# Thirty seven-product units in five downs, their first weight sum made in HBM by GpSimd's DMAs

## The chip, the core and the metric

The program runs on one core of one Trainium2 chip. The metric is the device time of one execution in microseconds, the median of three runs. A profiled execution gives the trace: its span is the time from the first to the last instruction, and its own time is given beside it.

## The reference, cut to what matters

Two transformer blocks follow one another on 256 tokens of width 1024, in float32. The first has a mixer (an RWKV part and a differential attention part, joined by gates), a feed-forward part with a squared ReLU and a gated embedding. The second has two layers, each with a half-weighted SwiGLU, an attention and a second half-weighted SwiGLU:

```python
x = x + jnp.square(jax.nn.relu(h @ w_ff1[i])) @ w_ff2[i]          # first block: 4096 rows of w_ff2
...
x = x + FFN_RES_WEIGHT * swiglu(rms_norm(x, norm_ffn1[layer]), ...)   # swiglu: (silu(x@gate) * (x@up)) @ down
x = x + mixed @ w_out[layer]
x = x + FFN_RES_WEIGHT * swiglu(rms_norm(x, norm_ffn2[layer]), ...)   # down: 2816 rows
```

The five long downs of the title are `w_ff2` (32 contraction tiles of 128) and the four `w_down` (22 tiles each); their output is 256 tokens by 1024 columns and is added to X.

## The kernel before, in words

**Pieces.** All weights stream through SBUF in the order of `stream_plan`, as pieces of 128 x 2048 float32 (1 MB). Piece j is loaded into `raw[j % 3]` by SyncE (`next_raw`, L3681), rounded to float32r on ScalarE into `hi[j % 3]` (L2688, script entry "hi"), and VectorE subtracts to get `lo[j % 3]` (L3067, entry "lo"). A product of activations and weights is three matmuls, high by high, high by low and low by high (`mm3`, L2179 to L2181). The cast of piece j waits until piece j-3 has been used, and the load of piece j+3 is issued when the low part of piece j is done. Each engine executes its entries in the order of one script, which a planner writes out when the program is built; the mixers and attentions are woven by it from several tracks, the feed-forward parts and downs run straight.

**A down.** `rows_into_x` takes the pieces of a down two contraction tiles at a time (pairs 0, 1, 2, ...), then two tail pieces of four tiles by 512 columns each. A pair is 256 rows of weights by 1024 columns, and the tokens come in two halves of 128: eight products of 128 tokens by 128 rows by 512 columns, 24 matmuls of 512 columns.

**Units.** For the pairs in `SEVENS` (`seven_piece`) the same result is made as a two by two block product with seven products (a Strassen-Winograd scheme) in place of eight. It needs three sums of activation blocks and three of weight blocks, each with a high and a low part:
- the token sums are made in the up projection or first feed-forward matrix, right after VectorE has the activations: `mix` (L3046 to L3051), a cast on ScalarE (L2673), `mix_lo` (L3059);
- the weight sums are made from the raw piece. With the piece's four blocks w0 to w3 of 512 columns, entry "w_sums" (L3086 to L3091) makes w3-w1, overwrites w1 in the raw buffer by w1-w0 (the block of product 5), then w3-(w1-w0) and w2 minus that. The piece's own cast therefore waits for the second of these four. ScalarE rounds the three sums (L2692, "w_hi"), VectorE subtracts (L3095, "w_lo").

The order of the products of a unit is "3127645", in the last unit of a down "1267543"; 6, 7 and 4 use the weight sums. Products 1, 5, 6 and 7 are accumulated over all units of a down in four banks of their own, and after the last unit `sevens_out` adds them into X (a copy on ScalarE, L2695, and eight instructions on VectorE, L3106 to L3124). The sums of weights lie in sets of buffers, two for the `w_down` ("a") and one for `w_ff2` ("s"), taken in turn; `used` makes a sum wait for the last unit of its set, and `after` for the matmuls that read what lay there before. In "a", `sums_early` emits the sums of the next unit before the low part of the piece ahead of it.

**GpSimd** does little: after each norm's squares it makes the reciprocal roots (entry "n_root", L3654 to L3660), for which VectorE waits at L3163 before it makes the rows of token factors. The first norm's root is made at 17 to 21 us, the second one's near 252 us, after the first mixer.

Of the kernel before, what the change touches and what calls it, by code (L numbers as in the profile page):

```python
# [30 lines left out]
SEVENS = {"a": (1, 3, 4, 6, 7), "s": (3, 5, 7, 9, 11)}  # L31
# [191 lines left out]
def program(nc, ws, xin, xtin, pin, colsin, constin, smallin, rowin, out):  # L223
# [4 lines left out]
    with ExitStack() as ctx:  # L228
# [10 lines left out]
        x_in = [[sem(f"x_in{b}{h}") for h in range(2)] for b in range(2)]  # L239
        raw_in = [sem(f"raw_in{i}") for i in range(NRAW)]  # L240
# [254 lines left out]
        class Sevens:  # L495


            def __init__(self, n, acts, sums, mixed, parts):
                self.H, self.L = acts
                self.sums = [(ar_([128, 3, 512], R), ar_([128, 3, 512], R), ar_.again([128, 3, 512])) for ar_ in sums]  # L500
                self.ML = [mixed([128, 3, 128], R) for _ in range(n)]
                self.MS = [mixed.again([128, 3, 128], i) for i in range(n)]
                self.MH = [mixed([128, 3, 128], R) for _ in range(n)]
                self.parts = [t[:, :, :].rearrange("p a n -> p (a n)") for t in parts]

        by_src = {"a": Sevens(5, (aH, aL), [Arena(14 * 4096), Arena(h_at - arena0)], Arena(17 * 4096), (sgm[0], sgm[1], sgs[0])),
                  "s": Sevens(5, (sH, sL), [Arena(h_at - arena0)], late_ar, (rl[0], rl[1], h_rest))}
# [5 lines left out]

        sevens = {}
        for i, (name, _, n, *_) in enumerate(plan):
            src = "a" if "_w_down_" in name else "s" if name == "w_ff2" else None
            if src and n // 2 in SEVENS[src]:
                sevens[i] = (src, SEVENS[src].index(n // 2))

# [90 lines left out]
        def emit_lo(j):  # L610
            if not weaving[0] and j + 1 in sevens and sevens[j + 1][0] == "a" and sevens[j + 1][1]:
                sums_early(j + 1)
            wanted["lo"].add(j)
            emit_wanted()
# [4 lines left out]
        def sums_early(j):  # L619

            if j in sevens and j not in summed:
                src, unit = sevens[j]
                sets = len(by_src[src].sums)
                in_h = unit == sets - 1
                summed[j] = [wsum_v.add() for _ in range(3)]
                emit("w_sums", dve=2.6, j=j, own=summed[j], used=sum(n < j for n in sevens) - min(unit, sets - 1),
                     after=freed[j - SEVENS[src][unit] - 1] if in_h else None)

        def split_hi():
# [3 lines left out]
            emit("hi", act=1.9, j=j, after=freed.get(j - NSPL), sums=summed[j][0] if j in sevens else None)  # L633
# [2015 lines left out]
        def scalar_program(e):  # L2649
# [27 lines left out]
            for s in script:  # L2677
                kind = s["kind"]
                sl = s.get("slot")
                if kind == "hi":  # L2680
                    j = s["j"]
                    e.wait_ge(raw_in[j % NRAW], 16 * (j // NRAW + 1))
                    if s["after"]:
                        e.wait_ge(s["after"][0], s["after"][1])
                    if s["sums"]:
                        e.wait_ge(wsum_v.sem, s["sums"])
# [310 lines left out]
        def vector_program(e):  # L2997
# [41 lines left out]
            def mix(mix_, a, made):  # L3039

                if mix_:
# [5 lines left out]
                    e.tensor_tensor(a[:, 0, second], a[:, 0, second], a[:, 1, second], ALU.add).then_inc(mix_v.sem, 1)  # L3047
# [3 lines left out]
                    e.tensor_tensor(z[:, 2, :], a[:, 1, first], z[:, 0, :], ALU.subtract).then_inc(mix_v.sem, 1)  # L3051
# [21 lines left out]
            for s in script:  # L3073
# [4 lines left out]
                elif kind == "w_sums":  # L3078
                    w = raw[s["j"] % NRAW][:, :].rearrange("p (q n) -> p q n", q=4)
                    e.wait_ge(raw_in[s["j"] % NRAW], 16 * (s["j"] // NRAW + 1))  # L3080
# [5 lines left out]
                    e.tensor_tensor(WS[:, 1, :], w[:, 3, :], w[:, 1, :], ALU.subtract)  # L3086
                    e.tensor_tensor(w[:, 1, :], w[:, 1, :], w[:, 0, :], ALU.subtract).then_inc(wsum_v.sem, 1)
                    e.wait_ge(wsum_v.sem, s["own"][0])
                    e.tensor_tensor(WS[:, 0, :], w[:, 3, :], w[:, 1, :], ALU.subtract).then_inc(wsum_v.sem, 1)
                    e.wait_ge(wsum_v.sem, s["own"][1])  # L3090
                    e.tensor_tensor(WS[:, 2, :], w[:, 2, :], WS[:, 0, :], ALU.subtract).then_inc(wsum_v.sem, 1)  # L3091
# [4 lines left out]
                elif kind == "seven_add":  # L3096
# [13 lines left out]
                    t = e.scalar_tensor_tensor(to[0, 1], banks[five.b][:, :], f[0], to[0, 1], ALU.mult, ALU.add)  # L3110
                    t.then_inc(seven_v.sem, 1)
                    ready(seven)
                    e.wait_ge(seven_v.sem, v[0])
                    e.tensor_tensor(w, banks[seven.b][:, :], u, ALU.add).then_inc(seven_v.sem, 1)
                    t = e.scalar_tensor_tensor(to[1, 1], banks[five.b][:, :], f[1], to[1, 1], ALU.mult, ALU.add)
                    t.then_inc(seven_v.sem, 1)
                    e.wait_ge(seven_v.sem, v[1])
                    t = e.scalar_tensor_tensor(to[0, 1], u, f[0], to[0, 1], ALU.mult, ALU.add)
                    t.then_inc(seven_v.sem, 1)
                    e.wait_ge(seven_v.sem, v[2])  # L3120
                    t = e.scalar_tensor_tensor(to[1, 0], w, f[1], to[1, 0], ALU.mult, ALU.add)
                    t.then_inc(seven_v.sem, 1)
                    e.wait_ge(seven_v.sem, v[3])
                    t = e.scalar_tensor_tensor(to[1, 1], w, f[1], to[1, 1], ALU.mult, ALU.add)  # L3124
# [500 lines left out]
        def gpsimd_program(e):  # L3625
# [20 lines left out]

            after_own(e.memset(st[:, 16:18], -0.5))
            for s in script:
                kind = s["kind"]
                sl = s.get("slot")  # L3650
                if kind == "n_root":
# [8 lines left out]
                    e.tensor_tensor(st[:, 14:16], st[:, 4:6], st[:, 4:6], ALU.mult).then_inc(factors.sem, 1)  # L3660
                elif kind == "f_roots":
# [13 lines left out]
        def sync_program(e):  # L3675
            def next_raw(j):

                if j + NRAW < len(plan):
                    i = j % NRAW
                    e.wait_ge(lo_ready, j + 1)  # L3680
                    e.dma_start(raw[i][:, :], ws[j + NRAW]).then_inc(raw_in[i], 16)  # L3681
# [126 lines left out]
```

## Time and profile before

| | |
|---|---|
| median of three runs | 1413.95 us (1413.87 to 1414.29) |
| the profiled execution's own time | 1413.19 us |
| its span | 1411.4 us |
| TensorE busy | 1403.6 us, 99% |
| VectorE, ScalarE, GpSimd busy | 1149.3 (81%), 817.8 (58%), 28.1 us (2%) |
| HBM read | 247.64 MB, 176 GB/s over the span |

Busy time is the union of an engine's instructions. Matmuls overlap in the trace (each is drawn 0.39 us long while the next starts earlier), so the price of a matmul is the distance between two starts. "Idle before" is put down to the engine whose event came last.

### The profile page before, as it was taken

The numbers are of one execution on the slowest core, as the hardware profiler recorded it, in microseconds if no ns is written. First come the engines' busy times: TensorE is split into PE (matmuls) and PEld (weight loads), VectorE is DVE, ScalarE is ACT, GpSimd is POOL, SyncE is SP. The second block draws the span as 40 slices with busy tenths as digits, with TensorE's granted clock in tenths as the row PEclk, the third lists the DMA queues.
The fourth block names the chain that finished last, engine by engine and source line by source line (L and its number), as shares of the span: only waits on it lengthen the run. The fifth ranks groups of instructions, "written<-read, shape, count | busy, mean of one in ns | idle before, by whom it ended". The sixth has DMA issues, their size and how long they took to land.

```text
span 1411.4 us, 22781 instructions
## 1 busy us (share of the span) xinstructions
PE 1403.6 (99%) x9163; PEld 1194.6 (85%) x9163; DVE 1149.3 (81%) x1601; ACT 817.8 (58%) x1110; POOL 28.1 (2%) x93
## 2 busy tenths in 40 slices
PE   8999999999999999999999999999999999999999
PEld 8988778888888888889878888888888887888887
DVE  6866776898877887988868888987889798688797
ACT  7745474655447655555766565555555557665562
POOL 1000000000001100000000000000000000000000
PEclk9999999999999999999999999999999999999999
DMA  9441325455555545455334555555545454355543
GB/s 357 163 150 63 115 102 203 179 179 209 199 211 179 209 180 192 167 207 200 135 117 176 182 199 187 209 179 190 198 179 201 163 176 147 113 203 191 182 176 120
DMA packets 37544, 250.15 MB, mean 177 GB/s; under 512 B 4288, under 2 KB 4416, under 8 KB 8384
## 3 DMA queue, kind: packets, MB, share of 16 engines
q1 hardware_dynamic: 37152, 248.51, 49.2%
q8 instruction: 73, 1.20, 0.3%
q10 hardware_dynamic: 288, 0.19, 0.1%
q14 instruction: 31, 0.25, 0.1%
HBM read 247.64 MB, written 1.05 MB: 176 GB/s over the span
## 4 chain that ended last, share of the span: by engine, by line
PE 97%; DMA 1%; ACT 0%; DVE 0%; SPq 0%; issue 0%; DVEq 0%; ACTq 0%
PE ps L2260 24%; PE ps L2179 16%; PE ps L2181 16%; PE ps L2180 15%; PE ps L2267 13%; PE ps L2432 2%; PE ps L2244 1%; PE ps L2248 1%; PE ps L2250 1%; DMA raw<-ws 1%; PE ps L2344 1%; PE ps L2645 1%; PE ps L2625 1%; PE ps L2634 1%; PE ps L2417 0%; PE ps L2569 0%
## 5 line engine op out<-in xcount | busy, mean ns | idle before, releaser
L3067 DVE TENSOR_TENSOR lo<-raw,hi 128x2048 fp32r<-128x2048 f32 (+1 forms) x230 | 522.3, 2271 | 61.1 <-ACT hi L2688 58.3
L2688 ACT CAST hi<-raw 128x2048 fp32r<-128x2048 f32 (+1 forms) x230 | 436.5, 1898 | 189.5 <-PE ps L2181 123.4
L2260 PE MATMUL ps<-h,hi 128*128 128x512 f32 x1504 | 359.0, 390 | 0.0
L2260 PEld LDWEIGHTS ps<-h,hi 128*128 128x128 f32 x1504 | 276.4, 188 | 52.5
L2179 PE MATMUL ps<-hi,a 128*128 128x512 f32 x516 | 204.7, 397 | 0.0
L2181 PE MATMUL ps<-hi,a 128*128 128x512 f32 x516 | 201.5, 390 | 0.0
L2180 PE MATMUL ps<-lo,a 128*128 128x512 f32 x516 | 201.1, 390 | 0.0
L2267 PEld LDWEIGHTS ps<-h,lo 128*128 128x128 f32 x1504 | 192.2, 190 | 7.9
L2267 PE MATMUL ps<-h,lo 128*128 128x256 f32 x1504 | 194.4, 282 | 0.0
L2892 ACT COPY a<-ps 128x256 f32<-128x256 f32 x208 | 76.1, 372 | 156.1 <-PE ps L2260 84.4
L3035 DVE TENSOR_TENSOR a<-ps,a 128x256 f32<-128x256 f32 x208 | 82.2, 419 | 41.8 <-ACT a L2892 41.6
L2179 PEld LDWEIGHTS ps<-hi,a 128*128 128x128 f32 x516 | 96.9, 188 | 21.6 <-issue 2.4
L2181 PEld LDWEIGHTS ps<-hi,a 128*128 128x128 f32 x516 | 96.9, 188 | 20.9
L2180 PEld LDWEIGHTS ps<-lo,a 128*128 128x128 f32 x516 | 97.0, 188 | 19.2
L2179 PE MATMUL ps<-hi,h 128*128 128x512 f32 x272 | 112.0, 412 | 0.0
L2181 PE MATMUL ps<-hi,h 128*128 128x512 f32 x272 | 106.3, 391 | 0.0
L2180 PE MATMUL ps<-lo,h 128*128 128x512 f32 x272 | 106.2, 390 | 0.0
L2179 PEld LDWEIGHTS ps<-hi,h 128*128 128x128 f32 x272 | 51.1, 188 | 12.2 <-issue 2.3
L2181 PEld LDWEIGHTS ps<-hi,h 128*128 128x128 f32 x272 | 51.0, 188 | 11.1
L2180 PEld LDWEIGHTS ps<-lo,h 128*128 128x128 f32 x272 | 51.3, 188 | 8.6
L2179 PE MATMUL ps<-h,hi 128*128 128x256 f32 x192 | 55.5, 289 | 0.0
L2712 ACT CAST h<-nt 128x512 fp32r<-128x512 f32 x32 | 19.8, 620 | 61.2 <-DVE nt L3149 60.9
(379 smaller groups left out, 1826.7 us busy)
## 6 DMA issues: line engine op xcount, KB each, us to landing
raw<-ws SPq DMA_DIRECT2D x227, 1024.0 KB, 4.8
raw<-ws SPq DMA_DIRECT2D x4, 512.0 KB, 8.1
X<-xin SPq DMA_DIRECT2D x8, 256.0 KB, 7.2
raw<-ws SPq DMA_DIRECT2D x4, 256.0 KB, 5.4
out<-X SPq DMA_DIRECT2D x4, 256.0 KB, 2.1
const<-const SPq DMA_DIRECT2D x1, 900.0 KB, 7.4
a<-xtin SPq DMA_DIRECT2D x3, 256.0 KB, 5.4
a<-row SPq DMA_DIRECT2D x1, 512.0 KB, 7.4
```

The lines of the kernel that those rows point to most:

```text
L2179: e.matmul(o, ah, bh, start=start, stop=False)
L2180: e.matmul(o, ah, bl, start=False, stop=False)
L2181: return e.matmul(o, al, bh, start=False, stop=stop)
L2244: t = e.matmul(b2(sl), wh[:, k, a:a + 128], h2[:, k, :, :], start=k == 0, stop=False)
L2260: t = e.matmul(b2(s["slots"][u]), wh[:, k, 128 * u:128 * u + 128], h2[:, k, :, :], start=k == 0, stop=last)
L2267: t = e.matmul(b2(s["slots"][u])[:, 0, :], wl[:, k, 128 * u:128 * u + 128], HH[:, k, :], start=False, stop=last)
L2432: t = e.matmul(banks[z.b][half(q ^ n), 64 * h:64 * h + 64], TB[blk][l][half(q), h, :], TB[blk][r][half(q), h, :], start=True, stop=True)
L2688: e.copy(hi[j % NSPL][:, n], raw[j % NRAW][:, n]).then_inc(hi_ready, 1)
L2712: e.copy(HH[:, 4 * h:4 * h + 4, 128 * b:128 * b + 128], n4[s["n"] % 2]).then_inc(h_hi.sem, 1)
L2892: e.copy(half_to[s["to"]][s["j"]][:, s["u"], :], b2(sl)[:, 1, :]).then_inc(half_a.sem, 1)
L3035: e.tensor_tensor(to[:, u, :], b2(x)[:, 0, :], half_to[kind][j][:, u, :], ALU.add).then_inc(free[x.b], 1)
L3067: e.tensor_tensor(lo[j % NSPL][:, n], raw[j % NRAW][:, n], hi[j % NSPL][:, n].bitcast(F), ALU.subtract).then_inc(lo_ready, 1)
```

## The change

The units become pairs 1, 3, 4, 5, 6, 7 in the four `w_down` (five before, without pair 5) and pairs 3, 5, 6, 8, 9, 11 in `w_ff2` (3, 5, 7, 9, 11 before): thirty units for 25. The signs of the scheme change (in `mix` too, not shown) so that the block of product 5 is w1+w0 and not w1-w0. This one sum is no longer made on VectorE: `make_sums` on GpSimd makes it for all thirty units in an HBM tensor, `block_sums`, in five groups of six. For each group it copies the second block of six pieces within HBM (256 KB each), waits for all six, adds the first block by six accumulating DMAs, and waits for those. It does so behind the first norm's root, once six low parts are done. The load of a unit's piece becomes three DMAs (w0, the sum, w2 and w3), and waits for the sum's group. VectorE's weight sums become three instructions for four, the piece's cast no longer waits for any of them, and the hint that emitted them early is gone. The sets of sums become three for "a" and two for "s", the new ones over buffers that are free by then. The eight instructions after the last unit stay eight, in another order.

```diff
@@ -28,7 +28,7 @@
 PARTS = (("Q1", "Q0", "K0", "K1", "V0", "V1"), ("Q1", "K1", "Q0", "V1", "K0", "V0"))
-SEVENS = {"a": (1, 3, 4, 6, 7), "s": (3, 5, 7, 9, 11)}
+SEVENS = {"a": (1, 3, 4, 5, 6, 7), "s": (3, 5, 6, 8, 9, 11)}
 HANDOVER = 0.2
@@ -497,25 +499,43 @@
                 self.H, self.L = acts
-                self.sums = [(ar_([128, 3, 512], R), ar_([128, 3, 512], R), ar_.again([128, 3, 512])) for ar_ in sums]
+                self.sums = [(low([128, 3, 512], R), high([128, 3, 512], R), low.again([128, 3, 512])) for low, high in sums]
                 self.ML = [mixed([128, 3, 128], R) for _ in range(n)]
...
-        by_src = {"a": Sevens(5, (aH, aL), [Arena(14 * 4096), Arena(h_at - arena0)], Arena(17 * 4096), (sgm[0], sgm[1], sgs[0])),
-                  "s": Sevens(5, (sH, sL), [Arena(h_at - arena0)], late_ar, (rl[0], rl[1], h_rest))}
+        def set_at(at_, high_at=None):
+
+            low = Arena(at_)
+            return low, low if high_at is None else Arena(high_at)
+
+        by_src = {"a": Sevens(6, (aH, aL), [set_at(14 * 4096), set_at(11 * 4096), set_at(h_at - arena0)], Arena(17 * 4096),
+                              (sgm[0], sgm[1], sgs[0])),
+                  "s": Sevens(6, (sH, sL), [set_at(h_at - arena0), set_at(0, 8 * 4096)], late_ar, (rl[0], rl[1], h_rest))}
...
             return by_src[src].sums[unit % len(by_src[src].sums)]
+
+        def made(j):
+
+            return j in sevens
+
+        def landed(j):
+
+            return 16 * sum(3 if made(n) else 1 for n in range(j % NRAW, j + 1, NRAW))
...
                 sevens[i] = (src, SEVENS[src].index(n // 2))
+        made_sums = sorted(sevens)
+        per_stage = len(SEVENS["a"])
+        assert len(SEVENS["s"]) == per_stage
+        block_sums = nc.dram_tensor("block_sums", (len(made_sums), 128, 512), F, kind="Internal").ap()
@@ -608,8 +628,6 @@
         def emit_lo(j):
-            if not weaving[0] and j + 1 in sevens and sevens[j + 1][0] == "a" and sevens[j + 1][1]:
-                sums_early(j + 1)
             wanted["lo"].add(j)
@@ -621,16 +639,22 @@
                 sets = len(by_src[src].sums)
-                in_h = unit == sets - 1
-                summed[j] = [wsum_v.add() for _ in range(3)]
+                first = j - SEVENS[src][unit]
+                if (src, unit) in (("a", 2), ("s", 0)):
+                    over = freed[first - 1]
+                elif (src, unit) == ("a", 1):
+                    over = (ff_v.sem, ff_v.n)
+                else:
+                    over = freed[first + 2] if (src, unit) == ("s", 1) else None
+                summed[j] = [wsum_v.add() for _ in range(2)]
                 emit("w_sums", dve=2.6, j=j, own=summed[j], used=sum(n < j for n in sevens) - min(unit, sets - 1),
-                     after=freed[j - SEVENS[src][unit] - 1] if in_h else None)
+                     after=over)
...
             sums_early(j)
-            emit("hi", act=1.9, j=j, after=freed.get(j - NSPL), sums=summed[j][0] if j in sevens else None)
+            emit("hi", act=1.9, j=j, after=freed.get(j - NSPL))
             if j in sevens:
@@ -2679,11 +2703,9 @@
                     j = s["j"]
-                    e.wait_ge(raw_in[j % NRAW], 16 * (j // NRAW + 1))
+                    e.wait_ge(raw_in[j % NRAW], landed(j))
                     if s["after"]:
                         e.wait_ge(s["after"][0], s["after"][1])
-                    if s["sums"]:
-                        e.wait_ge(wsum_v.sem, s["sums"])
                     n = slice(LAST_AT[j] if j < 3 else 0, PIECE)
@@ -3077,18 +3099,17 @@
                     w = raw[s["j"] % NRAW][:, :].rearrange("p (q n) -> p q n", q=4)
-                    e.wait_ge(raw_in[s["j"] % NRAW], 16 * (s["j"] // NRAW + 1))
+                    e.wait_ge(raw_in[s["j"] % NRAW], landed(s["j"]))
                     if s["used"]:
...
                     _, _, WS = sums_of(s["j"])
-                    e.tensor_tensor(WS[:, 1, :], w[:, 3, :], w[:, 1, :], ALU.subtract)
-                    e.tensor_tensor(w[:, 1, :], w[:, 1, :], w[:, 0, :], ALU.subtract).then_inc(wsum_v.sem, 1)
-                    e.wait_ge(wsum_v.sem, s["own"][0])
-                    e.tensor_tensor(WS[:, 0, :], w[:, 3, :], w[:, 1, :], ALU.subtract).then_inc(wsum_v.sem, 1)
-                    e.wait_ge(wsum_v.sem, s["own"][1])
-                    e.tensor_tensor(WS[:, 2, :], w[:, 2, :], WS[:, 0, :], ALU.subtract).then_inc(wsum_v.sem, 1)
+                    t = e.tensor_tensor(WS[:, 0, :], w[:, 3, :], w[:, 1, :], ALU.add)
+                    t.then_inc(wsum_v.sem, 1)
+                    e.wait_ge(wsum_v.sem, s["own"][-2])
+                    e.tensor_tensor(WS[:, 1, :], WS[:, 0, :], w[:, 0, :], ALU.subtract)
+                    e.tensor_tensor(WS[:, 2, :], w[:, 2, :], WS[:, 0, :], ALU.add).then_inc(wsum_v.sem, 1)
                 elif kind == "w_lo":
@@ -3107,21 +3128,19 @@
                     ready(five)
-                    t = e.scalar_tensor_tensor(to[0, 1], banks[five.b][:, :], f[0], to[0, 1], ALU.mult, ALU.add)
-                    t.then_inc(seven_v.sem, 1)
+                    e.wait_ge(seven_v.sem, v[0])
+                    e.tensor_tensor(copy, banks[five.b][:, :], u, ALU.subtract).then_inc(seven_v.sem, 1)
                     ready(seven)
-                    e.wait_ge(seven_v.sem, v[0])
                     e.tensor_tensor(w, banks[seven.b][:, :], u, ALU.add).then_inc(seven_v.sem, 1)
-                    t = e.scalar_tensor_tensor(to[1, 1], banks[five.b][:, :], f[1], to[1, 1], ALU.mult, ALU.add)
-                    t.then_inc(seven_v.sem, 1)
                     e.wait_ge(seven_v.sem, v[1])
-                    t = e.scalar_tensor_tensor(to[0, 1], u, f[0], to[0, 1], ALU.mult, ALU.add)
+                    t = e.scalar_tensor_tensor(to[0, 1], copy, f[0], to[0, 1], ALU.mult, ALU.add)
                     t.then_inc(seven_v.sem, 1)
                     e.wait_ge(seven_v.sem, v[2])
+                    e.tensor_tensor(u, banks[five.b][:, :], w, ALU.subtract).then_inc(seven_v.sem, 1)
                     t = e.scalar_tensor_tensor(to[1, 0], w, f[1], to[1, 0], ALU.mult, ALU.add)
                     t.then_inc(seven_v.sem, 1)
-                    e.wait_ge(seven_v.sem, v[3])
-                    t = e.scalar_tensor_tensor(to[1, 1], w, f[1], to[1, 1], ALU.mult, ALU.add)
+                    e.wait_ge(seven_v.sem, v[4])
+                    t = e.scalar_tensor_tensor(to[1, 1], u, f[1], to[1, 1], ALU.mult, ALU.add)
                     t.then_inc(seven_v.sem, 1)
@@ -3644,6 +3663,17 @@
+            def make_sums(groups):
+
+                for g in groups:
+                    units = range(per_stage * g, per_stage * g + per_stage)
+                    for n in units:
+                        e.dma_start(block_sums[n], ws[made_sums[n]][:, 512:1024]).then_inc(copied_out[g], 16)
+                    e.wait_ge(copied_out[g], 16 * per_stage)
+                    for n in units:
+                        e.dma_start(block_sums[n], ws[made_sums[n]][:, 0:512], accum_op=ALU.add).then_inc(sums_out[g], 16)
+                    e.wait_ge(sums_out[g], 16 * per_stage)
+
             after_own(e.memset(st[:, 16:18], -0.5))
@@ -3658,6 +3688,9 @@
                     e.tensor_tensor(st[:, 14:16], st[:, 4:6], st[:, 4:6], ALU.mult).then_inc(factors.sem, 1)
+                    if s["v"] == 1:
+                        e.wait_ge(lo_ready, 6)
+                        make_sums(range(5))
                 elif kind == "f_roots":
@@ -3678,7 +3711,14 @@
                     e.wait_ge(lo_ready, j + 1)
-                    e.dma_start(raw[i][:, :], ws[j + NRAW]).then_inc(raw_in[i], 16)
+                    if made(j + NRAW):
+                        n = made_sums.index(j + NRAW)
+                        e.wait_ge(sums_out[n // per_stage], 16 * per_stage)
+                        e.dma_start(raw[i][:, 0:512], ws[j + NRAW][:, 0:512]).then_inc(raw_in[i], 16)
+                        e.dma_start(raw[i][:, 512:1024], block_sums[n]).then_inc(raw_in[i], 16)
+                        e.dma_start(raw[i][:, 1024:2048], ws[j + NRAW][:, 1024:2048]).then_inc(raw_in[i], 16)
+                    else:
+                        e.dma_start(raw[i][:, :], ws[j + NRAW]).then_inc(raw_in[i], 16)
...
                 o = slice(512 * h, 512 * h + 512)

```

## Rows read from the trace of the kernel before

**Rows 1.** The page, busy time, share and instructions of each engine over the span.
```profile
PE 1403.6 (99%) x9163; PEld 1194.6 (85%) x9163; DVE 1149.3 (81%) x1601; ACT 817.8 (58%) x1110; POOL 28.1 (2%) x93
```

**Rows 2.** The table by stage: stretch, its length, each engine's busy time, clock, DMA share, GB/s.
```profile
30.00:260.00 230.00, 229.67 (x2792) 193.47 (x2791) 166.19 (x274) 129.74 (x206) 2.24 (x9) 1.00 0.38 137
260.00:1352.00 1092.00, 1092.00 (x5956) 931.26 (x5955) 915.50 (x1253) 643.44 (x860) 21.71 (x70) 1.00 0.51 183
420.00:575.00 155.00, 155.00 (x863) 135.11 (x862) 129.26 (x167) 96.23 (x132) 10.53 (x25) 1.00 0.52 184
507.40:518.50 11.10, 11.10 (x65) 9.82 (x64) 10.37 (x15) 6.67 (x9) 0.00 (x0) 1.00 0.49 186
518.50:529.60 11.10, 11.10 (x65) 9.82 (x64) 9.30 (x11) 6.37 (x8) 0.00 (x0) 1.00 0.53 190
529.60:540.70 11.10, 11.10 (x65) 9.83 (x64) 9.46 (x14) 6.67 (x9) 0.00 (x0) 1.00 0.56 193
```

**Rows 3.** The waits of TensorE: us in total, times, longest; the first of four entries.
```profile
PE ps L2186 <- DVE lo L3072: 1.4, 1, 1.4
```

**Rows 4.** Timeline of TensorE: a unit's products in `w_ff2`, and the next down's first matmul.
```profile
352.62 0.39 PE L2179 MATMUL ps<-a,a 128*128 128x512 f32 x1
...
353.30 0.39 PE L2179 MATMUL ps<-a,a 128*128 128x512 f32 x1
...
573.82 0.39 PE L2179 MATMUL ps<-hi,a 128*128 128x512 f32 x1
```

**Rows 5.** Timeline of VectorE in the second block's first down.
```profile
580.23 0.69 DVE L3086 TENSOR_TENSOR a<-raw 128x512 f32<-128x512 f32 x1
580.83 0.69 DVE L3087 TENSOR_TENSOR raw<-raw 128x512 f32<-128x512 f32 x1
581.56 0.69 DVE L3089 TENSOR_TENSOR a<-raw 128x512 f32<-128x512 f32 x1
...
582.89 0.68 DVE L3086 TENSOR_TENSOR a<-raw 128x512 f32<-128x512 f32 x1
...
585.55 2.28 DVE L3067 TENSOR_TENSOR lo<-raw,hi 128x2048 fp32r<-128x2048 f32 x1
587.75 1.75 DVE L3095 TENSOR_TENSOR a<-a,a 128x1536 fp32r<-128x1536 f32 x1
589.42 2.29 DVE L3067 TENSOR_TENSOR lo<-raw,hi 128x2048 fp32r<-128x2048 f32 x1
...
613.62 0.75 DVE L3106 SCALAR_TENSOR_TENSOR X<-a,st,X 128x512 f32<-128x512 f32 x1
...
618.12 0.75 DVE L3124 SCALAR_TENSOR_TENSOR X<-a,st,X 128x512 f32<-128x512 f32 x1
```

**Rows 6.** Groups of VectorE's instructions by line: the token sums, one of four and the low part.
```profile
L3059 DVE TENSOR_TENSOR a<-a,a 128x384 fp32r<-128x384 f32 x25 | 13.8, 551 | 0.0
L3046 DVE TENSOR_TENSOR a<-a 128x128 f32<-128x128 f32 x25 | 7.3, 293 | 0.9
```

**Rows 7.** The page's DMA issues: KB each, median us from issue to landing.
```profile
raw<-ws SPq DMA_DIRECT2D x227, 1024.0 KB, 4.8
...
X<-xin SPq DMA_DIRECT2D x8, 256.0 KB, 7.2
```

**Rows 8.** Timelines of VectorE, ScalarE and GpSimd in the first mixer and at its end.
```profile
30.30 2.29 DVE L3067 TENSOR_TENSOR lo<-raw,hi 128x2048 fp32r<-128x2048 f32 x1
...
61.49 2.28 DVE L3067 TENSOR_TENSOR lo<-raw,hi 128x2048 fp32r<-128x2048 f32 x1
...
74.09 1.92 ACT L2688 CAST hi<-raw 128x2048 fp32r<-128x2048 f32 x1 [5.49 <-PE ps L2181]
...
252.09 0.19 POOL L3654 TENSOR_TENSOR st<-st 128x2 f32<-128x2 f32 x1 [230.48 <-ACT ps L2723]
...
254.57 0.29 DVE L3163 TENSOR_SCALAR nt<-const,st 128x128 f32<-128x128 f32 x1 [2.46 <-POOL st L3640]
...
254.97 2.29 DVE L3067 TENSOR_TENSOR lo<-raw,hi 128x2048 fp32r<-128x2048 f32 x1
```

More of the change, by code:

```diff
@@ L239, in program @@
         x_in = [[sem(f"x_in{b}{h}") for h in range(2)] for b in range(2)]
+        copied_out = [sem(f"block_copied{g}") for g in range(5)]
+        sums_out = [sem(f"block_sums_out{g}") for g in range(5)]
         raw_in = [sem(f"raw_in{i}") for i in range(NRAW)]
@@ L3046, in mix @@
                     e.tensor_tensor(z[:, 1, :], a[:, 0, first], a[:, 0, second], ALU.subtract)
-                    e.tensor_tensor(a[:, 0, second], a[:, 0, second], a[:, 1, second], ALU.add).then_inc(mix_v.sem, 1)
+                    e.tensor_tensor(a[:, 0, second], a[:, 0, second], a[:, 1, second], ALU.subtract).then_inc(mix_v.sem, 1)
                     e.wait_ge(mix_v.sem, v[0])
@@ L3050, in mix @@
                     e.wait_ge(mix_v.sem, v[1])
-                    e.tensor_tensor(z[:, 2, :], a[:, 1, first], z[:, 0, :], ALU.subtract).then_inc(mix_v.sem, 1)
+                    e.tensor_tensor(z[:, 2, :], a[:, 1, first], z[:, 0, :], ALU.add).then_inc(mix_v.sem, 1)
             def mix_lo(mix_):
```

## The prediction

> **What bounds the kernel now.** I read the page first, then the table by stage, the waits of TensorE, the timeline of one down, and last the queues and GpSimd in the first mixer. The page gives TensorE 1403.6 of 1411.4 us; VectorE has 81%, ScalarE 58%, GpSimd 2% [rows 1]. The table by stage has the granted clock at 1.00 throughout and shows where TensorE is not busy: 0.3 us in the first mixer (30 to 260 us), nothing from 260 to 1352, and so the other 7.5 at the two ends [rows 2]. The list of TensorE's waits has four entries, none above the 1.4 us of its first, which is in the start [rows 3]. So a matmul taken away anywhere between 260 and 1352 us shortens the run by its own spacing, as long as no other engine becomes late. That is the whole question: five products are taken out of a full engine, and VectorE, ScalarE and the DMA queues get more or other work around them.
>
> **The gain on TensorE.** A pair of contraction tiles costs eight products of three matmuls in the plain form and seven in the other. Inside a down the first matmul of a product starts every 0.68 us (352.62, then 353.30), so one matmul takes 0.2267 us and one product 0.68 us [rows 4]. The change makes 30 units out of 25, one more in each of the five long downs: 5 x 0.68 = 3.40 us. Nothing else on TensorE changes in number.
>
> **VectorE in the four downs of the feed-forward blocks.** Here is the risk of the edit, because the units are now pairs 3 to 7 in a row and not 3, 4, 6, 7. In the second block's first down a unit's weight sums take four instructions, the first at 580.23; the third, which waits for the second's result, starts 0.73 after it (580.83 to 581.56), and the next unit's first is at 582.89: 2.66 us. The low part of the piece takes 2.20 (585.55 to 587.75), the low part of the sums 1.67 (587.75 to 589.42) [rows 5]. The new sums are three instructions: the second waits for the first's result, 0.73 as there, then 0.60 and 0.61, so 1.94 us. A unit then costs VectorE 1.94 + 2.20 + 1.67 = 5.81 us while TensorE takes 21 x 0.2267 = 4.76 us for it. VectorE loses 1.05 us on each of the units in a row, and lives from its lead.
>
> The lead can be counted. The down starts at 573.82 [rows 4]. Pair 0 is plain (24 x 0.2267 = 5.44), pair 1 a unit, 2 plain, 3 to 7 units: pair 3 starts at 589.46, then 594.22, 598.98, 603.74, and pair 7 at 608.50. VectorE comes to the sums of pair 3 at 580.23, as before, and can then run on: no sum waits for its buffers, since there are three sets and each is three units old, and each cast of ScalarE (1.9 us, released when pair j-3 is done) comes before the subtraction that needs it. Five units end at 580.23 + 5 x 5.81 + 0.08 = 609.36. Pair 7 begins with two products that need no sums, so its sums are wanted at 608.50 + 1.36 = 609.86; they come 0.5 us ahead. Its low part comes at 607.69 for 608.50, 0.8 ahead; pairs 3 to 6 have between 1.9 and 5.0. I take no stall, at a margin of 0.1 us per unit. Had the sums kept their 2.66 us, five units would end 3.6 us later, 3.1 us too late in each of four downs, 12 us in all: this is what the addition made in HBM pays for.
>
> After pair 7 the low part of pair 8 is ready at 611.6 for 613.26, and of the first tail piece at 613.8 for 618.7. The eight additions to X after the last unit are still eight; they ran from 613.62 to 618.9 [rows 5], and in this order again start near 613.8, so the second tail piece gets its low part near 621.8 for 624.1. The down of the first block has units 3, 5, 6, 8, 9, 11, at most two in a row, with a plain piece (TensorE 5.44, VectorE 2.20) after them; its two sets tie each sum to the end of pair j-3, which the cast waits for anyway. Five units there are ready 4 us or more before use: cost nothing.
>
> **The token sums.** One more unit needs in the up projection four instructions of 0.29 us and one of 0.55 on VectorE [rows 6], and a cast on ScalarE: some 1.7 us in a stage of 155 us where VectorE is busy 129 [rows 2]. In a pair of pieces (11.1 us) it is busy 9.5 us with such sums; the first down's up projection has one with additions to X beside it, 10.4, and the new sums fall into the one behind it, 9.3 and so 11.0 of 11.1 [rows 2]. A backlog of a few tenths ends in the next pair. Cost nothing.
>
> **The loads.** The piece of a unit is now three DMAs in SP's queue (256, 256 and 512 KB) for one. A 1 MB piece lands 4.8 us after its issue, and the 256 KB loads of X took 7.2 [rows 7]. In the row of units the load of pair j+3 is issued when the low part of pair j is done: for pair 6 at 584.5, wanted at 594.3; for pair 7 at 590.2, wanted at 599. Even 7 us are hidden. SP's new wait for the sums in HBM holds every later load behind it, but it first occurs near 320 us, so it costs only if GpSimd is that late.
>
> **HBM sums on GpSimd.** Sixty DMAs of 256 KB in ten batches, each waited for. They start when six low parts are done, at 32.6 (the end of the first row of [rows 8]), and GpSimd's next work is at 252.09 (L3654) [rows 8]: 219.5 us, or 21.9 us a batch. The trace has no copy within HBM and none that adds, so the price is bounded by loads. A batch is 1.5 MB, by the piece loads 1.5 x 4.8 = 7.2 us and ten of them 72; if each DMA took the slowest 7.2 us and none overlapped, 43 us a batch and 432 in all. A batch of six in flight is nearer to the first; doubled for the adding ones that read twice, 5 x 7.2 + 5 x 14.4 = 108 us, over by 141. I take that, and no cost. The Trainium skill (DMA: Bandwidth & Descriptors, Anatomy of one DMA, SWDGE path) fits one such DMA as about 2.0 us plus its bytes at 436 GB/s; an estimate by it for six in flight is 5.6 us a batch and 56 in all, and no run so far shows it.
>
> What they disturb meanwhile: from 30 to 260 us the DMA engines are busy 38% at 137 GB/s [rows 2]. The tightest load there is issued at 63.8 (end of the low part begun at 61.49) and cast at 74.09: 10.3 us for 4.8 [rows 8]. If half the engines' time goes to GpSimd's queue it lands in 9.6, still in time, and after the cast there are some more us before TensorE wants the piece. So 0 is the lower end; the upper is 4 us, if each of the dozen loads under way came 0.3 late and the mixer passed all of it on. I take 0.1, since the row is nearer to being in time.
>
> **The sum.** Profiled span 1411.4 - 3.40 + 0.1 = 1408.1; the profiled execution's own time is 1.8 above its span, so 1409.9. The median of the runs (1413.95) is 0.8 above that execution's 1413.19, which gives 1410.7 us. What a first GpSimd queue adds outside the span no row shows; 0 to 1 us, taken as 0.
>
> **Rivals.**
> - *The mixer pays part* (chance 0.22). GpSimd's transfers share the DMA engines with the loads, and the mixer's chains run over VectorE, busy 166 of its 230 us, with TensorE full beside it [rows 2]. For it: TensorE has hardly a gap there, so any chain that comes late shows. Against: 10 us of room per load. 0.5 to 4 us lost, 1411.2 to 1414.5. The Trainium skill (SBUF — State Buffer, Who interferes with whom) says that a DMA issued from GpSimd can be starved of port time by VectorE's two-port modes, and that a two-input tensor_tensor is measured not to do so; by that rule VectorE's subtractions slow neither side, and no run so far shows it.
> - *VectorE is late in the row of units* (0.10). It decides from 0.1 us more per unit: with d more, 4 x (5d - 0.5) us; d = 0.3 costs 4.0 us and gives 1414.7.
> - *Slower: GpSimd is not done at 252 us* (0.12). Adding DMAs are much slower than loads, or are issued one by one. Then the root of the second norm is late, VectorE stands before L3163 (at 254.57, itself waiting 2.46 us for it), and behind it the low part at 254.97, without which TensorE stops some 5 us later (an estimate) [rows 8]. It decides from 22.5 us a batch on, and each us more costs 10: 24 us a batch lose 15 and give 1426.
> - *Better* than the forecast's own range (0.03).
>
> **Numbers.** The forecast (1409.9 to 1411.4) has 0.53. The range for 8 in 10 takes in the mixer's cost and most of the VectorE rival: 1409.8 to 1414.8. About 0.2% (2.8 us) is what a measurement of this kernel can tell from no change, so faster means below 1411.1, which is only 0.4 us above the forecast. Faster are 0.50 of the forecast's 0.53, the better case's 0.03 and 0.03 of the mixer's: 0.56. The same are the forecast's other 0.03, 0.18 of the mixer's and 0.07 of VectorE's: 0.28. Slower are all of GpSimd's 0.12, 0.03 of VectorE's and 0.01 of the mixer's: 0.16.
>
> **What would show it.** Right: TensorE's gaps stay at 7.8 us, a down of a feed-forward block is 0.68 us shorter, VectorE's last sums of it end about 0.5 us before the third product of pair 7, and L3654 starts near 252. Wrong: an entry of TensorE waiting for VectorE in a down, casts waiting for the loads between 33 and 150 us, or GpSimd's first addition after 252 us.

## The result and the profile after

The changed kernel takes 1422.5 us (median of 13 runs, 1416.8 to 1425.3) against 1413.95 us before (13 runs beside it, 1413.1 to 1415.0). The ratio is 1.0058, interval 1.0051 to 1.0065: slower, outside the range of the forecast. Its profiled execution took 1417.9 us with a span of 1416.1, so the trace shows 4.7 us of the loss: it is the second fastest of the thirteen. The changed kernel's runs spread over 8.5 us, those of before over 1.9.

From the page after: the busy times (answering to [rows 1]), the DMA queues and three issue lines.
```profile
PE 1402.2 (99%) x9148; PEld 1193.2 (84%) x9148; DVE 1156.1 (82%) x1621; ACT 828.8 (59%) x1120; POOL 69.4 (5%) x153
...
q1 hardware_dynamic: 45792, 248.51, 49.7%
q0 software_dynamic: 6720, 15.73, 5.2%
q8 instruction: 73, 1.20, 0.4%
...
block_sums<-ws POOLq DMA_DIRECT2D x60, 256.0 KB, 7.2
raw<-ws SPq DMA_DIRECT2D x34, 256.0 KB, 3.4
raw<-block_sums SPq DMA_DIRECT2D x30, 256.0 KB, 3.8
```
TensorE's gaps are 13.9 us instead of 7.8. Queue q0 is GpSimd's; q8 brings instructions, 73 packets of 16 KB over the whole run. By their number they are TensorE's: the trace records 18,808 of its instructions (matmuls, weight loads and semaphore instructions), 258 to a packet.

The waits of TensorE after, the first seven entries (before: [rows 3]).
```profile
PE ps L2456 <- issue: 3.6, 2, 2.8
PE ps L2230 <- ACT hi L2723: 1.5, 1, 1.5
PE ps L2466 <- issue: 1.2, 1, 1.2
PE ps L2210 <- DVE lo L3094: 1.4, 1, 1.4
PE ps L2230 <- DVE h L3157: 1.1, 1, 1.1
PE ps L2397 <- ACT a L2770: 0.8, 1, 0.8
PE ps L2203 <- issue: 0.4, 1, 0.4
```
No entry belongs to a down. New are three entries put to "issue", 5.2 us: TensorE stood, and no semaphore held it.

Where the time goes can be read from rows that both kernels have. First GpSimd's timeline after: its batches and the second norm's root, which was at 252.09 [rows 8].
```profile
33.29 3.39 POOL L3671 DMA_DIRECT2D block_sums<-ws  x6 [11.49 <-DVE lo L3089]
48.91 5.07 POOL L3674 DMA_DIRECT2D block_sums<-ws  x6 [12.23 <-DMA block_sums<-ws]
...
94.70 3.15 POOL L3671 DMA_DIRECT2D block_sums<-ws  x6 [14.46 <-DMA block_sums<-ws]
...
151.46 5.02 POOL L3674 DMA_DIRECT2D block_sums<-ws  x6 [5.26 <-DMA block_sums<-ws]
260.37 0.19 POOL L3684 TENSOR_TENSOR st<-st 128x2 f32<-128x2 f32 x1 [103.89 <-ACT ps L2745]
```
GpSimd has issued its last batch 104 us before the root, and the last packet of its queue is through at 166.6 us; the root waits for ScalarE and comes 8.28 us late. The eight roots by their line, before and then after, with the times of the first and the last:
```profile
L3654 POOL TENSOR_TENSOR st<-st x8: 193/194/197, 17.2 to 1233.9; 128x2 f32<-128x2 f32 x8
```
```profile
L3684 POOL TENSOR_TENSOR st<-st x8: 188/194/196, 17.3 to 1239.3; 128x2 f32<-128x2 f32 x8
```
The last root is 5.4 us late and the end 4.7. So all the loss is made before 260 us, and behind it the five downs give back 8.28 - 4.7 = 3.6 us, the 3.4 that the prediction worked out.

Where in the mixer? The low parts of the weight pieces in VectorE's timeline, before and then after.
```profile
93.21 2.29 DVE L3067 TENSOR_TENSOR lo<-raw,hi 128x2048 fp32r<-128x2048 f32 x1 [1.72 <-ACT hi L2688]
112.58 2.28 DVE L3067 TENSOR_TENSOR lo<-raw,hi 128x2048 fp32r<-128x2048 f32 x1
121.87 2.29 DVE L3067 TENSOR_TENSOR lo<-raw,hi 128x2048 fp32r<-128x2048 f32 x1 [2.24 <-ACT hi L2688]
143.31 2.29 DVE L3067 TENSOR_TENSOR lo<-raw,hi 128x2048 fp32r<-128x2048 f32 x1 [3.21 <-ACT hi L2688]
```
```profile
93.58 2.29 DVE L3089 TENSOR_TENSOR lo<-raw,hi 128x2048 fp32r<-128x2048 f32 x1 [1.72 <-ACT hi L2710]
112.96 2.28 DVE L3089 TENSOR_TENSOR lo<-raw,hi 128x2048 fp32r<-128x2048 f32 x1
126.82 2.29 DVE L3089 TENSOR_TENSOR lo<-raw,hi 128x2048 fp32r<-128x2048 f32 x1 [2.24 <-ACT hi L2710]
151.55 2.29 DVE L3089 TENSOR_TENSOR lo<-raw,hi 128x2048 fp32r<-128x2048 f32 x1 [3.21 <-ACT hi L2710]
```
The shift is 0.37, 0.38, 4.95 and 8.24 us. The first 0.4 us is there at 30 us, before GpSimd's first transfer at 33; the rest is two losses, 4.6 us behind 113 and 3.3 us before 151. The idle times in brackets are the same, so no cast and no load came later relative to its surroundings.

The first loss in TensorE's timeline after, and the same burst before.
```profile
110.69 0.91 PE L2456 MATMUL ps<-a,a 64*64 64x64 f32 x45
114.38 0.90 PE L2456 MATMUL ps<-a,a 64*64 64x64 f32 x19 [2.78 <-issue]
```
```profile
110.32 1.24 PE L2432 MATMUL ps<-a,a 64*64 64x64 f32 x64
```
A burst of 64 small matmuls, which depend on nothing new, breaks off after 45. The table by stage of the same stretch, after (columns as in [rows 2]):
```profile
112.00:114.40 2.40, 0.02 (x3) 0.02 (x4) 2.29 (x6) 1.87 (x8) 0.00 (x0) 1.00 0.98 142
114.40:118.00 3.60, 3.60 (x28) 3.10 (x29) 2.50 (x8) 1.66 (x3) 0.00 (x0) 0.53 1.08 235
118.00:120.00 2.00, 2.00 (x16) 1.39 (x16) 0.00 (x0) 0.00 (x0) 0.78 (x2) 1.00 0.83 314
```
After standing 2.78 us TensorE works 3.6 us at a granted clock of 0.53, nearly its lower level of 1.2 GHz; that costs another 0.47 x 3.6 = 1.7 us, and 2.8 + 1.7 = 4.5 us is nearly all of the first loss. The second has pauses of 0.4, 1.2 and 0.9 us and no fall of the clock. They leave 0.8 of its 3.3 us, which lies at the same three places, as the count of instructions below shows.

What TensorE stood for, the DMA packets of 108 to 112 us show, before and then after:
```profile
q8 instruction: 1, 0.02, 1.5%
```
```profile
q0 software_dynamic: 352, 0.65, 101.6%
```
Before, the DMA engines were all but empty and an instruction packet passed at 108.5. After, they are full with GpSimd's transfers and none passes; it comes in the slot 112.0 to 112.5, and TensorE goes on at 114.38.

### The profile page after: what moved, and what is told of

It is laid out like the page before. It is cut to its first block, busy times and chain, and to the rows that moved or that the text cites. A ratio compares the mean times of both kernels' runs of the same rounds, so it can differ in the third digit from the quotient of the medians.

```text
span 1416.1 us, 22943 instructions
## 1 busy us (share of the span) xinstructions
PE 1402.2 (99%) x9148; PEld 1193.2 (84%) x9148; DVE 1156.1 (82%) x1621; ACT 828.8 (59%) x1120; POOL 69.4 (5%) x153
## 4 chain that ended last, share of the span: by engine, by line
PE 97%; DMA 1%; issue 1%; ACT 0%; DVE 0%; SPq 0%; DVEq 0%; ACTq 0%
PE ps L2284 24%; PE ps L2203 16%; PE ps L2205 15%; PE ps L2204 15%; PE ps L2291 13%; PE ps L2456 2%; PE ps L2268 1%; PE ps L2272 1%; PE ps L2274 1%; DMA raw<-ws 1%; PE ps L2368 1%; PE ps L2669 1%; PE ps L2649 1%; PE ps L2658 1%; PE ps L2441 0%
## 5 line engine op out<-in xcount | busy, mean ns | idle before, releaser
L2203 PE MATMUL ps<-hi,a 128*128 128x512 f32 x496 | 196.8, 397 | 0.0
L2205 PE MATMUL ps<-hi,a 128*128 128x512 f32 x496 | 193.6, 390 | 0.0
L2204 PE MATMUL ps<-lo,a 128*128 128x512 f32 x496 | 193.3, 390 | 0.0
L2203 PEld LDWEIGHTS ps<-hi,a 128*128 128x128 f32 x496 | 93.2, 188 | 20.6 <-issue 2.4
L2205 PEld LDWEIGHTS ps<-hi,a 128*128 128x128 f32 x496 | 93.1, 188 | 20.0
L2204 PEld LDWEIGHTS ps<-lo,a 128*128 128x128 f32 x496 | 93.2, 188 | 18.4
L2714 ACT CAST a<-a 128x1536 fp32r<-128x1536 f32 x30 | 44.6, 1485 | 38.0 <-DVE a L3112 38.0
## 6 DMA issues: line engine op xcount, KB each, us to landing
const<-const SPq DMA_DIRECT2D x1, 900.0 KB, 10.6
```

The source lines that it names most:

```text
L2203: e.matmul(o, ah, bh, start=start, stop=False)
L2204: e.matmul(o, ah, bl, start=False, stop=False)
L2205: return e.matmul(o, al, bh, start=False, stop=stop)
L2714: e.copy(WH[:, :, :], WS[:, :, :]).then_inc(wsum_a.sem, 1)
```

## The experiments

The kernel before ran beside each: its medians are 1413.9 us for the first four experiments, 1414.1 for the next four and 1413.9 for the last three.

**Only the traffic.** The kernel before with all sixty transfers, their sums unused:

```diff
+                    if s["v"] == 1:
+                        e.wait_ge(lo_ready, 6)
+                        make_sums(range(5))
```


> The kernel before with GpSimd's sixty HBM transfers added and nothing else: the sums are made and not used, loads and units are those of before. Theory A (the mixer is lost to GpSimd's traffic itself; TensorE stands between 110 and 150 us in its bursts of 64x64 matmuls because its instructions come late): the whole loss without the gain of the units, 1413.95 + 8.5 + 3.6 = about 1426 us, with idle of TensorE put to 'issue' in those bursts and none elsewhere. Theory B (the loss comes with the new loads in three DMAs or with SP's wait): within 1 us of before, 1413 to 1415. Theory C (VectorE or the loads of the mixer are slowed): slower too, but with waits of TensorE for VectorE or ScalarE, or casts waiting for the loads.


Measured 1425.5 us (1422.3 to 1427.7), ratio 1.0080 (1.0067 to 1.0092): the transfers alone cost 11.6 us in the median, 11.8 in the profiled spans. Of the 11.8, 1.1 us are there at 30 us, before the first transfer; in the other traces it is 0 to 0.9 us there, whatever the edit. Its waits of TensorE:
```profile
PE ps L2439 <- issue: 7.1, 3, 2.8
...
PE ps L2449 <- issue: 0.9, 1, 0.9
```

**Only the units.** The changed kernel without the transfers within HBM; the sum is left out, and product 5 takes the plain second block.

```diff
-                        make_sums(range(5))
...
-                        e.wait_ge(sums_out[n // per_stage], 16 * per_stage)
...
-                        e.dma_start(raw[i][:, 512:1024], block_sums[n]).then_inc(raw_in[i], 16)
+                        e.dma_start(raw[i][:, 512:1024], ws[j + NRAW][:, 512:1024]).then_inc(raw_in[i], 16)
```


> The changed kernel without GpSimd's transfers; the middle load of a unit's piece reads the plain second block from the weights, so the sum of two blocks is left out and product 5 and the weight sums use the plain block. Theory A: the mixer is as before and the units give what the trace showed behind it (3.6 us), so 1410.4 us, second root near 252.1. Theory B: the loss of 8.5 us stays, above 1420.


Measured 1410.5 us (1409.9 to 1411.3), ratio 0.9975 (0.9966 to 0.9985), no pause put to issue. The rest of the change gains 3.4 us; the two parts add up (11.6 - 3.4 = 8.2 for a measured 8.5).

**Only early.** The kernel before with the first two groups, over near 95 us.

```diff
-                        make_sums(range(5))
+                        make_sums(range(2))
```


> The kernel before with only the first two of the five groups (24 transfers, over by some 95 us). Theory A (the bursts of small matmuls from 108 us on are what suffers): no more than 1 us over before, 1413.5 to 1415. A price by the byte (2/5 of the whole) would give about 4.8 us, 1418.8.


Measured 1414.1 us, ratio 1.0002 (0.9992 to 1.0011). 40% of the bytes cost nothing there, so the price is not one by the byte.

**Only late.** The last three groups, from the fifteenth low part (95.5 us) on.

```diff
+                        e.wait_ge(lo_ready, 15)
+                        make_sums(range(2, 5))
```


> The kernel before with only the last three groups (36 transfers), begun when fifteen low parts are done, at 95.5 us. Theory A: all of the loss of the run with all five groups, about 1426 us, within 2 us of that run. A price by the byte (3/5): 1421.


Measured 1420.9 us (1419.5 to 1424.7), ratio 1.0050 (1.0038 to 1.0063). Most of the price is in this place: 7.0 us. That it would reach the 11.6 of the first experiment is missed, and 1421 is what a price by the byte gives; that price is ruled out by the early run, not by this one. Why it falls short is not tested. Its six batches lie at other moments, and its trace has two pauses (2.2 and 1.4 us) for the four of the first experiment.

**Later in the changed kernel.** Group 1 as in the change, the other four behind the second norm's root.

```diff
-                        make_sums(range(5))
+                        make_sums(range(1))
+                    elif s["v"] == 2:
+                        make_sums(range(1, 5))
```


> The changed kernel with only the first group of sums in the first mixer and the other four behind the second norm's root, from 252 to about 360 us, beside feed-forward matmuls 256 and 512 columns wide. Theory A (instructions of TensorE come late, which costs only where it uses up many small matmuls): nothing is lost, 1410.5 us as without the sums, no idle of TensorE between 260 and 1352 us. Theory C (whatever shares the DMA engines with this traffic is slowed, the piece loads above all): the loads of that stretch, 183 GB/s against 137 in the mixer, come late and 3 to 8 us are lost, 1413.5 to 1418.


Measured 1410.4 us (1409.8 to 1411.8), ratio 0.9975 (0.9965 to 0.9984): the whole computation, faster than both kernels. In its profile the last accumulating batch is issued at 364 us, and TensorE's gap in the mixer is 0.6 us where it was 0.3:
```profile
30.00:260.00 230.00, 229.37 (x2790) 193.19 (x2790) 166.26 (x273) 129.19 (x205) 13.92 (x27) 1.00 0.46 152
260.00:1352.00 1092.00, 1092.00 (x5957) 931.63 (x5956) 924.29 (x1277) 655.05 (x870) 51.58 (x112) 1.00 0.57 194
```

**Without accumulating.** As "only late", the second half plain copies (the edit is shown against "only late").

```diff
-                        e.dma_start(..., ws[summed_pieces[n]][:, 0:512], accum_op=ALU.add)
+                        e.dma_start(..., ws[summed_pieces[n]][:, 0:512])
```


> The three groups in the bursts as before, but the adding transfers made plain copies of the same blocks. If any GpSimd transfer in rows of 2 KB delays the instructions, the loss stays at 5 to 8 us (1419 to 1422). If the adding ones are what does it (TensorE's longest pause began beside them), it falls under 2 us.


Measured 1420.0 us (1419.9 to 1422.5), ratio 1.0047 (1.0035 to 1.0060). Accumulating is not what costs.

**One in flight.** 24 transfers from 95 us on, each waited for before the next (again against "only late"; the adding half has the same two new lines).

```diff
                         e.dma_start(block_sums[n], ws[summed_pieces[n]][:, 512:1024]).then_inc(copied_out[0], 16)
+                        at += 16
+                        e.wait_ge(copied_out[0], at)
```


> Twenty-four transfers from 95 us on, copies and adding ones, each waited for, so that one is in flight and not six. Theory A with a queue (the instructions wait behind what is already queued in the 16 DMA engines): a wait can be no longer than one transfer, and the loss falls from 7 us to under 1.5 us, below 1415.5. If the mere presence of the traffic does it, 24 of 36 transfers cost about 4 to 5 us.


Measured 1415.0 us (1414.1 to 1418.9), ratio 1.0011 (1.0002 to 1.0020), one pause of 0.3 us in the trace, which is of the fastest run. In the median a single transfer costs little; 14 of the 24 lay between 95 and 165 us, so the bytes there were fewer as well.

**Long rows.** The bytes of three groups as plain copies in rows of 8 KB for 2 KB.

```diff
+                        e.dma_start(copies[0], ws[summed_pieces[2 * g + half]]).then_inc(copied_out[0], 16)
+                        e.dma_start(copies[1, 0:64], ws[summed_pieces[2 * g + half + 6], 0:64]).then_inc(copied_out[0], 16)
```


> Plain copies of the same bytes as the three groups (six batches of 1.5 MB from 95 us on) in rows of 8 KB in place of 2 KB. If short rows are what fills the DMA engines, the batches are over sooner and the loss is under 3 us; if only the bytes in flight count, as with the 2 KB copies.


Measured 1422.7 us (1420.4 to 1423.2), ratio 1.0058 (1.0045 to 1.0070), pauses of 1.4, 1.4 and 2.9 us and a granted clock of 0.83 from 140 to 160. Fewer, longer rows don't help.

**Queue against queue, place against place.** The last three have the same 36 plain copies of 256 KB in six batches. Two issue them at the same six low parts between 95 and 165 us, behind SyncE's load or from GpSimd; the third issues them from GpSimd between 188 and 240 us. Shown are SyncE's edit in `next_raw`, GpSimd's behind the first root, and the third against the second.

```diff
+                    if 15 <= j + 1 < 21:
+                        for n in range(6 * (j - 14), 6 * (j - 13)):
+                            e.dma_start(copies[n], ws[summed_pieces[n % 30]][:, 512:1024]).then_inc(copied_out, 16)
```


> The kernel before with 36 plain copies of 256 KB between HBM tensors, in six batches of 1.5 MB at the times of the six weight loads between 95 and 165 us, issued by SyncE right behind its own load, on its queue; the copies are read by nobody. Theory A (any dense traffic on the DMA engines beside the bursts of 64x64 matmuls holds back TensorE's instruction packets): 1418 to 1423 us, with pauses put to issue. Rival B (only the queue of GpSimd does that, through its descriptors or its own lane): 1413.5 to 1414.5 us and no pause over 0.5 us. Between, 1415 to 1417, would leave both in part.


```diff
+                        for g in range(6):
+                            e.wait_ge(lo_ready, 15 + g)
+                            for n in range(6 * g, 6 * g + 6):
+                                e.dma_start(copies[n], ws[summed_pieces[n % 30]][:, 512:1024]).then_inc(copied_out, 16)
```


> The same 36 copies at the same six moments, issued by GpSimd. A and B both: 1417 to 1422 us with pauses put to issue of 1 to 3 us each, since six copies at once from GpSimd gave 1420.0 us at other moments. Should it lie within 0.2% of 1414 us, then the moments of the batches decide and not the queue, and the comparison with the run from SyncE's queue says nothing.


```diff
-                            e.wait_ge(lo_ready, 15 + g)
+                            e.wait_ge(lo_ready, (22, 23, 25, 27, 28, 30)[g])
```


> The same 36 copies from GpSimd, at six moments between 188 and 240 us, where TensorE runs 7 matmuls in a microsecond and not 20 or more. Theory A (instruction packets are needed too often only in the bursts of small matmuls): 1413.5 to 1415 us, no pause put to issue over 0.5 us. Rival C (dense copies cost TensorE time wherever they lie while loads run beside them): 1417 us or more.


Measured, in this order: 1417.2 us (1416.1 to 1419.3), ratio 1.0024 (1.0015 to 1.0034); 1418.2 us (1417.6 to 1419.5), 1.0029 (1.0018 to 1.0041); 1413.9 us (1413.5 to 1414.4), 0.9998 (0.9989 to 1.0008). The first is 0.8 us below what the traffic theory had expected, but far from the 1413.5 to 1414.5 of its rival: either queue does it, and the intervals of the two overlap. Of the second, the time is in the expected range, but only one of its four pauses (1.8 us) is of the expected 1 to 3 us. The place decides: the same copies cost 4.3 us or nothing.

Their waits put to issue, from SyncE and then from GpSimd in the bursts; behind the bursts there is none.
```profile
PE ps L2185 <- issue: 1.1, 1, 1.1
...
PE ps L2438 <- issue: 0.4, 1, 0.4
```
```profile
PE ps L2185 <- issue: 2.2, 2, 1.8
...
PE ps L2438 <- issue: 0.9, 2, 0.7
```
What the traces show to differ between the places is how many instructions TensorE takes. The table by stage of the last kernel, a stretch without its copies and the one with them:
```profile
125.00:140.00 15.00, 15.00 (x413) 12.56 (x412) 10.41 (x32) 5.31 (x16) 0.00 (x0) 1.00 0.22 74
...
180.00:260.00 80.00, 79.64 (x468) 64.43 (x467) 58.26 (x70) 47.82 (x61) 21.08 (x45) 1.00 0.74 264
```
The first has 413 matmuls and 412 weight loads in 15 us, 55 a microsecond; the second 12 a microsecond, and there DMA engines busy 74% harm nobody. The instruction queue's packets say the same. Kernel before, stretches 30 to 95, 95 to 165 and 180 to 260 us:
```profile
q8 instruction: 5, 0.08, 0.4%
```
```profile
q8 instruction: 12, 0.20, 1.3%
```
```profile
q8 instruction: 4, 0.07, 0.3%
```
One packet in 13 us, in 5.8 and in 20: only in the bursts is the next one wanted that soon.

I looked for the instruction packet in front of each pause put to issue, in slots of 0.5 us, in the changed kernel and in the seven experiments with copies in the bursts. In all 23 cases one lies 2.2 to 2.9 us before TensorE goes on, counted from the start of its slot, while packets are 3.4 to 10 us apart. One more pause, of 0.3 us, stands in the "later" kernel at 111.67 us with no copies beside it and 3.2 us behind its packet: the supply is close to short there anyway. By the packets' own times all 24 pauses end 1.2 to 1.5 us after the end of a packet. For the longest pause of the changed kernel it is this row, of 112.0 to 112.5:
```profile
q0 software_dynamic: 37, 0.07, 84.1%
q8 instruction: 1, 0.02, 13.3%
```

**Where in TensorE's stream.** Count TensorE's recorded instructions from the start, in order of time. In front of the first one behind each pause lie, in all 24 cases and in kernels whose pauses come at quite different times, 2241, 2498, 3010, 3266, 3521, 3777 or 4545 instructions: steps of 256, or of multiples of it, within one. That is the length of a 16 KB packet by the count above. So TensorE stands only where one packet's instructions end and the next one's begin, whatever the instruction there is (a matmul of a burst or one of 512 columns).

The same count shows where all of the loss lies, since TensorE's instructions are the same in every kernel up to there. Subtract the start of each in the trace of before from its start in the other: from 95 to 165 us the difference grows at these places, and in the stretches at the lower clock; between them it changes by less than 0.1 us over any twelve instructions. In the changed kernel it grows by 3.05, 0.70, 1.38 and 1.12 us at 2498, 3010, 3521 and 3777, and by 1.6 at the lower clock, 7.9 in all; these steps are 0.2 to 0.3 us longer than the pauses listed above, and so take in the 0.8 us left over there. With SyncE's copies 2.6 of 2.7 us lie at four such places, with GpSimd's all 4.1. With the early traffic there is no step, and with the copies behind the bursts one of 0.3 us at 2498, as without any transfers.

## Why the prediction was wrong

The step that failed is **"What they disturb meanwhile"**, taken at 0.1 us with an upper bound of 4. Alone the transfers cost 11.6 us. The step asked only whether the weight loads still land in time, and on that it was right: no cast waited longer. It took the loads for the only thing that the DMA engines carry. They also carry TensorE's instructions, in 12 packets between 95 and 165 us, and while the engines are full these come late. The pauses are short, but TensorE is full there and each is lost whole; behind most of the long ones comes the lower clock.

- **The gain on TensorE**: 3.40 us; measured 3.6 in the spans behind the mixer and 3.4 by the experiment with only the units. Right.
- **VectorE in the four downs**: 5.81 us a unit, no stall. The first and last sums of the five units after, in VectorE's timeline (columns as in [rows 5]):
```profile
587.30 0.69 DVE L3108 TENSOR_TENSOR a<-raw 128x512 f32<-128x512 f32 x1
...
593.11 0.69 DVE L3108 TENSOR_TENSOR a<-raw 128x512 f32<-128x512 f32 x1
...
610.52 0.69 DVE L3108 TENSOR_TENSOR a<-raw 128x512 f32<-128x512 f32 x1
```
593.11 - 587.30 = 5.81 us, and no down has a wait of TensorE. Right, and that rival falls.
- **The token sums** and **the loads**: 0. The parts of a split piece land in 3.4, 3.8 and (the 512 KB) 4.6 us in the median, and TensorE is busy for all of 260 to 1352 us but 0.04. Right.
- **HBM sums on GpSimd**: 7.2 us for a copying and 14.4 for an adding batch, over by 141 us. Measured from start to start, the copying ones take 8.4 to 15.6 us, 10.6 in the mean, the adding ones 13.8 to 19.5, and GpSimd's queue is empty by 168 us: slower than taken, and still 84 us ahead of 252. Near enough, and the rival in which GpSimd isn't done at 252 us falls. The estimate of 5.6 us a batch by the page's fit is too low by a factor of 1.5 to 3.5.
- **The mixer pays part** named the place and not the way: it had the loads and VectorE's chain late, at 0.5 to 4 us. Neither was, and the price of the transfers, 7.9 to 11.6 us, is two to three times its upper end. VectorE's low parts took 2.28 to 2.29 us beside the transfers as without them (the rows above).
- **The sum**: with the measured 11.6 in place of 0.1 it gives 1410.7 + 11.5 = 1422.2 us, for a measured 1422.5.

Shown are the place, that either queue does it, that rows, accumulation and bytes as such do not, that all pauses lie where a block of TensorE's instructions ends, and that each ends 1.2 to 1.5 us after the packet with instructions. No experiment delayed instruction packets alone, but I know of no other cause that would keep to these places. How the traffic holds a packet back is not shown. Open is why the runs of the changed kernel spread over 8.5 us (which burst meets a full stretch may differ from run to run).

The Trainium skill bears on this in two places. Runtime: NRT & Kernel Launch (Instruction fetch mechanics) says that each engine's instructions are streamed in blocks of 16 KiB, 256 instructions, over a DMA queue, at a cost that is mostly hidden. The trace agrees with the block (73 packets, 1.20 MB, and pauses 256 instructions or multiples of it apart) and, while the DMA engines are quiet, with the hiding; it doesn't hold for 55 instructions a microsecond beside full engines. DMA: Bandwidth & Descriptors (Queues, rings and completion order) says that a DMA engine goes round the queues it has work for, a packet at a time. From that one would expect that a queue with little to carry waits its turn behind others; the runs agree in that the copies harm from SyncE's queue as from GpSimd's, and hardly with one in flight, but show no single turn.

## What to carry to other kernels

Before traffic is put into a stretch where "the DMA engines are idle anyway", count TensorE's instructions a microsecond there and look at the instruction queue in the table of queues: where packets pass every 6 us, batches of six 256 KB transfers stopped TensorE for 0.2 to 2.8 us at a time. Put such traffic where TensorE runs long matmuls (here four of the five groups, begun behind 255 us in place of 65, turned +8.5 us into -3.7), or keep a single transfer in flight. A wait put to "issue" in the middle of a burst, with no semaphore, is the mark to look for, and so are pauses whose places in TensorE's stream lie multiples of 256 instructions apart.

## What the runs showed of the hardware

- TensorE's instructions came in 73 packets of 16 KB over the same DMA engines as everything else; transfers from HBM to HBM stopped TensorE for up to 2.9 us at a time, always at places of its stream that lie multiples of 256 instructions apart, and it went on 1.2 to 1.5 us after the packet's end.
- After 2.78 us of standing the granted clock was 0.53 for 3.6 us; after pauses of 1.2 and 0.9 us it stayed at 1.00. The length of the pause alone doesn't decide it: of the six pauses above 2 us in all traces five (2.2 to 2.9 us) had the lower clock behind them, and one of 2.78 us, in "only the traffic", had not. Its row, from when TensorE went on:
```profile
115.10:117.60 2.50, 2.50 (x30) 2.17 (x31) 2.39 (x8) 1.56 (x3) 1.84 (x4) 1.00 0.28 52
```
- An accumulating batch of six within HBM took 13.8 to 19.5 us, a copying one 8.4 to 15.6; its issue alone took GpSimd 5.07 us against 3.15.
